# A two-layer encoder step on one core: statistics in two products at feed-forward norms, half chunks of low parts at norms, the last centrings on TensorE

## The reference

```python
h = layer_norm_0(alpha * h + 0.5 * swiglu_0(h))               # norms 0 and 3
h = layer_norm_1(alpha * h + concat(A(h), B(h), C(h), D(h)) @ w_o)   # norms 1 and 4
h = layer_norm_2(alpha * h + 0.5 * swiglu_1(h))               # norms 2 and 5
# swiglu: (silu(h @ w_gate) * (h @ w_up)) @ w_down, with 2816 hidden features
# layer_norm: (x - mean) * rsqrt(var + 1e-5) * g + b, over the 1024 features
```

## Time and profile before

| | |
|---|---|
| median of 3 runs | 1159.66 us (1159.55 to 1159.9) |
| profiled execution | 1159.8 us, span 1158.0 us |
| busy: TensorE | 1131.5 us, 98% of the span |
| busy: VectorE, ScalarE, GpSimd | 688.5, 542.7, 95.5 us |
| mean granted TensorE clock | 0.996 |

### The profile page before, as it was taken

How to read it: one execution, slowest core, us unless ns; L and a number is a source line. 1 busy time by engine, 2 the same in 40 slices (tenths; PEclk the granted TensorE clock), 3 DMA queues, 4 the chain that set the end, 5 groups by cost and what they waited for, 6 DMA issues and landing times.

```text
span 1158.0 us, 20727 instructions
## 1 busy us (share of the span) xinstructions
PE 1131.5 (98%) x8612; PEld 1098.8 (95%) x8612; DVE 688.5 (59%) x929; ACT 542.7 (47%) x770; POOL 95.5 (8%) x92
## 2 busy tenths in 40 slices
PE   9999999999998999999999999999999989999996
PEld 8999999979898999999999999999788989999995
DVE  5545545777659754445584545467867596454443
ACT  6343443464655634344464344346547564434432
POOL 1000000100153000000100000010003610000001
PEclk9999999999999999999999999999999999999998
DMA  9554444433333544444445454452433325544431
GB/s 344 183 182 149 168 158 159 149 129 99 120 125 135 179 153 177 151 158 164 147 162 199 149 181 136 164 171 95 166 114 126 127 91 201 179 150 169 164 101 41
DMA packets 28020, 177.02 MB, mean 153 GB/s; under 512 B 3312, under 2 KB 3376, under 8 KB 10288
## 3 DMA queue, kind: packets, MB, share of 16 engines
q1 hardware_dynamic: 26208, 170.18, 43.1%
q0 software_dynamic: 1744, 5.88, 1.4%
HBM read 171.79 MB, written 4.25 MB: 152 GB/s over the span
## 4 chain that ended last, share of the span: by engine, by line
PE 88%; DVE 5%; ACT 3%; issue 2%; DMA 1%; POOL 1%; SPq 0%; DVEq 0%; POOLq 0%; ACTq 0%
PE ps L475 25%; PE ps L476 25%; PE ps L477 25%; ACT w_high L1092 1%; PE ps L512 1%; PE ps L517 1%; PE ps L513 1%; DMA raw<-weights 1%; DVE w_low L1407 1%; DVE z L1559 1%; PE ps L907 1%; PE ps L906 1%; PE ps L908 1%; PE ps L864 1%; PE ps L603 1%
## 5 line engine op out<-in xcount | busy, mean ns | idle before, releaser
L475 PE MATMUL ps<-x_high,w_high 128*128 128x288 f32 x1536 | 456.3, 297 | 2.5 <-DVE w_low L1407 2.0
L1407 DVE TENSOR_TENSOR w_low<-raw,w_high 128x2048 fp32r<-128x2048 f32 (+4 forms) x151 | 328.9, 2180 | 211.0 <-ACT w_high L1092 210.6
L477 PE MATMUL ps<-x_high,w_low 128*128 128x288 f32 x1536 | 452.9, 295 | 0.0
L476 PE MATMUL ps<-x_low,w_high 128*128 128x288 f32 x1536 | 452.8, 295 | 0.0
L1092 ACT ACTIVATE w_high<-raw 128x2048 fp32r<-128x2048 f32 (+2 forms) x166 | 302.7, 1827 | 113.8 <-PE ps L477 109.1
L475 PEld LDWEIGHTS ps<-x_high,w_high 128*128 128x128 f32 x1536 | 288.5, 188 | 6.2 <-DVE w_low L1407 2.5
L477 PEld LDWEIGHTS ps<-x_high,w_low 128*128 128x128 f32 x1536 | 288.4, 188 | 0.0
L476 PEld LDWEIGHTS ps<-x_low,w_high 128*128 128x128 f32 x1536 | 288.2, 188 | 0.2
L477 PE MATMUL ps<-hid_high,w_low 128*128 128x288 f32 x704 | 208.2, 296 | 0.0
L476 PE MATMUL ps<-hid_low,w_high 128*128 128x288 f32 x704 | 208.2, 296 | 0.0
L475 PE MATMUL ps<-hid_high,w_high 128*128 128x288 f32 x704 | 208.1, 296 | 0.0
(11 more groups left out here) (311 smaller groups left out, 1141.2 us busy)
## 6 DMA issues: line engine op xcount, KB each, us to landing
raw<-weights SPq DMA_DIRECT2D x138, 1024.0 KB, 4.9
raw<-weights SPq DMA_DIRECT2D x16, 768.0 KB, 4.3
raw<-weights SPq DMA_DIRECT2D x4, 968.0 KB, 5.1
raw<-weights SPq DMA_DIRECT2D x6, 512.0 KB, 4.0
raw<-weights SPq DMA_DIRECT2D x8, 256.0 KB, 5.9
out_k<-kT POOLq DMA_DIRECT2D x2, 864.0 KB, 4.5
raw<-weights SPq DMA_DIRECT2D x2, 640.0 KB, 5.6
hT<-x_in SPq DMA_DIRECT2D x4, 288.0 KB, 5.3
```

The costliest lines, as they stand in the source:

```text
L475: pe.matmul(out, wh, xh, start=first, stop=False, skip_group_check=True)
L476: pe.matmul(out, wh, xl, start=False, stop=False, skip_group_check=True)
L477: return pe.matmul(out, wl, xh, start=False, stop=last, skip_group_check=True)
L1407: dve.tensor_tensor(wl, r, wh.bitcast(F32), ALU.subtract).then_inc(low_ready, 1)
```

## The change

- At norms 0, 2 and 3 (`sums_whole`) VectorE adds slice 7 to the sum of slices and its square to the sum of squares, and TensorE makes two products instead of four. At the mixers' norms four stay, with the mean's two ahead of the squares'.
- `EARLY_FFN` is 2 instead of 1, `EARLY_MIX` 2 instead of 3.
- In `norm`, VectorE makes only half of the next low part between the variance and the first scaled slice, and the other half after slice 3 (norms 0, 3) or 4 (norms 1, 2, 4). TensorE waits for the halves singly.
- At the mixers' norms: VectorE, not GpSimd, makes the low part of the first feed-forward chunk, ahead of slices 0 and 1. The two columns are made before any slice. The half chunk that stood after slices 2 and 3 stands ahead of slices 4 and 5; the early low parts of slices 2 and 3 move behind slice 7. ScalarE makes early high parts ahead of squares, and the third chunk's high part ahead of the mean's square.
- Norm 5: ScalarE copies minus the mean here too. TensorE centres slices 3 to 7 with two identity products each (`center_last`), and VectorE scales them from PSUM.
- The activation table of the feed-forward block is loaded at the very start, not after the first high parts.

```diff
-POOL_LOW = tuple(range(WO_AT, FFN1_AT + 1))
+POOL_LOW = tuple(range(WO_AT, FFN1_AT))
-EARLY_FFN, EARLY_MIX = 1, 3
+EARLY_FFN, EARLY_MIX = 2, 2
+BY_DVE = 3
...
+            return n in EARLY and n % 3 != 1          # sums_whole(n)
...
-                low(l, WO_AT + 4)                      # GpSimd
...
@@ TensorE, stats(n)
                 pe.wait_ge(zsum_ready, n + 1)
+                if sums_whole(n):
+                    pe.matmul(mean, ones, zsum[:, 0, :], start=True, stop=True).then_inc(mean_ready, 1)
+                    pe.wait_ge(all_squares_ready, whole_before(n) + 1)
+                    pe.matmul(square, ones, zsqsum[:, 0, :], start=True, stop=True).then_inc(stat_ready, 1)
+                    for k in range(first, KD):
+                        early_tile(n, k)
+                    return
...
+            def center_last():
+                for j in range(BY_DVE, KD):
+                    out = ps[:, last_bank(j), 0:TOK]
+                    pe.matmul(out, ident, z[:, j, :], start=True, stop=False, skip_group_check=True)
+                    if j == BY_DVE:
+                        pe.wait_ge(mean_copied, len(EARLY) + 1)
+                    pe.matmul(out, ident, minus_mean[:, :], start=False, stop=True, skip_group_check=True)\
+                        .then_inc(last_centered, 1)
...
@@ ScalarE, square(n, q), at mixers
+                        if n % 3 == 1:
+                            high_until(next_chunks(n) + NSPLIT)
@@ ScalarE, norm(n)
+                act.activation(minus_mean[:, :], stat_banks(n)[0], ACT.Copy, scale=-1.0 / D_MODEL).then_inc(mean_copied, 1)
                 if n in EARLY:
-                    act.activation(minus_mean[:, :], stat_banks(n)[0], ACT.Copy, scale=-1.0 / D_MODEL).then_inc(mean_copied, 1)
...
@@ VectorE, residual(n, q, used, after)
                 if n % 3 == 1:
                     dve.wait_ge(part_added, 4 * (n // 3) + q + 1)
+                    if q == 2:
+                        low_half(after, 0)
+                        dve.wait_ge(wo_ready, 2 * (n // 3) + 2)
...
+                    if at_ == 7 and sums_whole(n):
+                        dve.wait_ge(z_ready, 5 * (n + 1))
+                        dve.tensor_tensor(zsum[:, 0, :], zsum[:, 0, :], z[:, 7, :], ALU.add).then_inc(zsum_ready, 1)
+                        dve.wait_ge(zsqsum_ready, n + 1)
+                        dve.wait_ge(zsq_ready, 5 * (n + 1))
+                        dve.tensor_tensor(zsqsum[:, 0, :], zsqsum[:, 0, :], zsq[:, 1, :], ALU.add)\
+                            .then_inc(all_squares_ready, 1)
                 if q == 3:
                     if n % 3 == 1:
+                        early_low(n, 1)
                         early_low(n, 2)
                     early_low(n, 3)
                     low_half(after, 1)
...
-                if n % 3 == 1 and q == 1:
-                    low_half(after, 0)
-                if n % 3 != 1 or q == 1:
+                if n % 3 != 1:
                     early_low(n, q)
@@ VectorE, norm(n)
                 center(0)
                 center(1)
                 if n in EARLY:
-                    low_until(next_chunks(n) + NSPLIT)
+                    low_half(next_chunks(n) + 2, 0, half_low_ready)
                 dve.wait_ge(rstd_ready, n + 1)
                 scale(0)
                 high_first()
+                if n not in EARLY:
+                    for j in range(2, BY_DVE):
+                        center(j)
+                    for j in range(1, KD):
+                        scale(j)
+                    return
                 scale(1)
                 for j in range(2, KD):
                     center(j)
                     low(j - 2)
                     scale(j)
+                    if n in EARLY and j == (3 if which == 0 else 4):
+                        low_half(next_chunks(n) + 2, 1)
...
@@ VectorE, mixer(l)
-                low_until(base + MIX_CHUNKS + WO_CHUNKS + 1)
                 out_low(l, 2)
                 copy_t(l, 2)
                 part(l, 3)
                 out_low(l, 3)
+                dve.wait_ge(columns_ready, l + 1)
+                early_columns(3 * l + 1)
+                low_until(base + MIX_CHUNKS + WO_CHUNKS + 1)
```

More of the change, by code:

```diff
@@ L313, in down_bank, with last_bank, sums_whole, whole_before @@
             return (6, 4)[q % 2]
+        def last_bank(j):
+            return (0, 1, 6, 7, 4)[j - BY_DVE]
+        def sums_whole(n):
+            return n in EARLY and n % 3 != 1
+        def whole_before(n):
+            return sum(sums_whole(m) for m in range(n))
         def squares_added(n, q):
@@ L1065, in _ @@
                 stats(3 * l + 2)
+            center_last()
         @block.scalar
@@ L1141, in early_high, with early_columns @@
                                    scale=gb[:, n // 3, n % 3, 0, j:j + 1]).then_inc(zx_high_ready, 1)
+            def early_columns(n):
+                return act.activation(zx_high[:, :, TOK:ZW].rearrange("p k c -> p c k"), gb[:, n // 3, n % 3, :, :], ACT.Copy)
             def square(n, q):
                 act.wait_ge(z_ready, 5 * n + q + 1)
-                if q == 0:
+                if q == 0 and n % 3 == 1:
+                    early_high(n, 0)
+                    early_high(n, 1)
+                    act.activation(zsqsum[:, :, :], z[:, 0:2, :], ACT.Square).then_inc(zsq_ready, 1)
+                elif q == 0:
                     act.activation(zsqsum[:, :, :], z[:, 0:2, :], ACT.Square).then_inc(zsq_ready, 1)
@@ L1150, in square @@
                     if n in EARLY:
-                        act.activation(zx_high[:, :, TOK:ZW].rearrange("p k c -> p c k"), gb[:, n // 3, n % 3, :, :], ACT.Copy)
+                        early_columns(n)
                     early_high(n, 0)
@@ L1357, in mixer @@
                     square(3 * l + 1, q)
+            act.preload_act_table_set("silu_and_others")
             for pair in range(4):
@@ L1407, in low_part, with low_half @@
                 dve.tensor_tensor(wl, r, wh.bitcast(F32), ALU.subtract).then_inc(low_ready, 1)
-            def low_half(c, half):
+            def low_half(c, half, signal=None):
                 if c >= DEPTH * LAYER_CHUNKS:
@@ L1423, in low_half @@
                     split[0] += 1
+                elif signal is not None:
+                    ins.then_inc(signal, 1)
             def ffn(l, i):
@@ L1533, in early_low @@
                     dve.wait_ge(const_landed, 8 * 16)
-                if q == 0:
+                if q == 0 and which != 1:
                     dve.wait_ge(zx_high_ready, KD * early_before(n) + 1)
-                    dve.tensor_tensor(zx_low[:, :, TOK:ZW].rearrange("p k c -> p c k"), gb[:, l, which, :, :],
-                                      zx_high[:, :, TOK:ZW].rearrange("p k c -> p c k").bitcast(F32), ALU.subtract)
+                    early_columns(n)
                 for j in (2 * q, 2 * q + 1):
@@ L1548, in center @@
                 def center(j):
[L1550 to L1554, removed]
-                def scale(j):
-                    dve.wait_ge(centered, KD * n + j + 1)
-                    dve.scalar_tensor_tensor(out=z[:, j, :], in0=z[:, j, :], scalar=gb[:, l, which, 0, j:j + 1],
+                    dve.tensor_tensor(z[:, j, :], minus_mean[:, :], z[:, j, :], ALU.add).then_inc(centered, 1)
+                def scale(j):
+                    if n in EARLY or j < BY_DVE:
+                        dve.wait_ge(centered, KD * n + j + 1)
+                        x = z[:, j, :]
+                    else:
+                        dve.wait_ge(last_centered, j - BY_DVE + 1)
+                        x = ps[:, last_bank(j), 0:TOK]
+                    dve.scalar_tensor_tensor(out=z[:, j, :], in0=x, scalar=gb[:, l, which, 0, j:j + 1],
                                              in1=rstd[:, :], op0=ALU.mult, op1=ALU.mult).then_inc(norm_ready, 1)
```

48 lines of the change are left out of this document (34 added, 14 removed).

## The result

The changed kernel takes 1152.82 us in the median of 4 runs (1152.5 to 1153.11), the kernel before 1159.78 beside it: a ratio of 0.994, 95% interval 0.9924 to 0.9956. It is faster by 7.0 us; the forecast was 5.1, 1154.6. The time lies in the forecast's wide range (1152.5 to 1157.2), 0.3 above its lower end, and outside the narrower one that the forecast called its own (1153.6 to 1155.8). The profiled execution took 1153.06 us, span 1151.3.

A forecast was written before the change was run, and what follows sets the result against it. TensorE bounds the kernel, with an equally long VectorE path to the fifth chunk behind norms 1, 2 and 4. Terms 1.3 - 0.15 + 1.5 + 2.45 = 5.1 off 1159.66 give 1154.6 us; range 1152.5 to 1157.2, own 1153.6 to 1155.8.

The forecast's parts named there:

- The main idea: Behind norms 1, 2 and 4 VectorE's variance to fifth chunk, 24.2 us, is a second path as long as TensorE's.
- Norms 0 and 3: Two statistics products fewer save TensorE 0.97; first scaled slice comes 0.7 earlier; gain 0.65 each, bounds 0 and 0.97.
- The rotation: In the mixer behind norms 0 and 3, 1.15 of shift meets some 1.15 of slack at the first rotation product.
- Norm 2: Feed-forward to feed-forward: fifth chunk ready 0.27 later against 0.12 of slack, a loss of 0.15; bounds -0.5 and +0.3.
- Norm 5: The tail: five of eight centrings go to TensorE as ten identity products; gain 2.45, bounds 1.9 and 2.9.
- Rival (d): In the tail TensorE's clock falls to 1.2 GHz, identity products take 0.97 each: 1158.8, no change; chance 0.07.
- Norms 1 and 4: Mixer to feed-forward: VectorE takes GpSimd's 2.29 low part, yet variance comes 0.6 to 0.7 earlier; gain 0.75 each.
- the stretched price: At the mixers' norms VectorE's half chunk of low parts takes 2.50 beside GpSimd's sum, instead of 1.22 alone.
- (a): Mixers' norms give nothing: GpSimd's sums stretch early low parts too, or ScalarE's high part is late; 1156.1, chance 0.16.
- (b): Halved statistics products give nothing or cost: -0.4 for norm 2, 0 for the others; 1156.1, chance 0.16.
- (c): TensorE's idle time at mixers is wholly won, 3.3 each, as ScalarE and VectorE catch up; 1149.5, chance 0.06.
- (e): Slower: low part taken from GpSimd delays the mixers' chain by its full 2.29, 3.2 a norm; 1162.5, chance 0.05.

The follow-up runs named there:

- The late half: Changed kernel with the third chunk's whole low part between VectorE's variance and first scaled slice, instead of half there and half later: 1154.54 us.
- the shorter way: Way from variance to fifth chunk shortened behind norms 1, 2 and 4: 1149.25 us on the changed kernel, 1159.97 on the kernel before.
- norm 2's products: Norm 2 back to four statistics products and one early tile: 1152.58 us on the changed kernel, 1150.25 on the one with the shortened way.

## Why the forecast came out as it did

**The main idea held.** Behind norms 1, 2 and 4 the way over VectorE and ScalarE to the fifth chunk was as long as TensorE's. The late half (no loss there, 0.96 at norms 0 and 3), the shorter way (3.4 on one kernel, 0.2 on the other) and norm 2's products (nothing, or 0.96) each show it from another side. The stalls of 0.6 came where the forecast put them. That the total stayed within the range is in part luck: the mixers' norms won 3.4 together, where the range's lower end gave them 2.0, and the other norms and the start stayed below what that end gave them.

**Norms 0 and 3:** forecast 0.65 each, won 0.83 and 0.80, within the bounds. That is 0.15 short of the two products' 0.97, with a wait of 0.3 for the first low part of x (line 929 in the waits, 0.6 for two norms) as the forecast had it: TensorE is there 0.97 earlier, the slice a little less. The rotation had enough slack. Undone alone, the products cost 0.66 there and the half 0.96, together twice what the change won: without either edit the other wins little, so here too two ways had to be shortened together.

**Norm 2:** forecast -0.15, measured -0.21. That two products fewer win nothing there was right; that the numbers are so close is luck. The forecast's own terms give a fifth chunk 0.5 - 0.27 = 0.23 later, not 0.27. In the trace the variance is 0.40 later, but the low part behind it only 0.04 (4.85 behind slice 7 instead of 4.81), as that waited for ScalarE before; its two halves cost another 0.05 over the whole. The fifth chunk's low part and first matmul, kernel after:

```profile
598.10 2.29 DVE L1462 TENSOR_TENSOR w_low<-raw,w_high 128x2048 fp32r<-128x2048 f32 x1 [1.35 <-ACT w_high L1133]
```
```profile
600.53 0.40 PE L490 MATMUL ps<-x_high,w_high 128*128 128x288 f32 x1
```

With slice 7 at 573.12, and at 574.96 before, the low part starts 24.98 behind it instead of 24.89, 0.09 later. Its end and TensorE's first matmul are 0.14 apart here, where TensorE waited for it (the 0.22 without a name, above), and 0.18 before; so the slack was 0.04 rather than 0.12. Both terms were too large, and 0.12 of the measured loss lies behind the gating, where the forecast had nothing.

**Norm 5:** forecast 2.45, won 2.54, 2.53 by the run that undid it. Rival (d), a lower clock in the tail, didn't come: from 1141.5 to the end the granted clock was 1.00, the 2.4 GHz level, where it had been 0.63 behind TensorE's end.

**Norms 1 and 4: the step that failed is one price.** "I take the stretched price, as GpSimd starts some 0.6 us into it: 356.4" is the mis-sized term. The half took 1.23, not 2.50: the price was taken from a row in which GpSimd had started first, for a walk in which VectorE starts first. The walk up to it was right: with the 0.21 between the kernels added, slices 0 and 1 came at 349.58 (forecast 349.7) and the half at 353.83 (354.0). Then slices 4 and 5 came at 354.98 (356.4). The sum behind them gave back 0.45, as GpSimd now waits for the half and so falls on the sum; slice 7 came at 359.0 (359.95), and the variance at 363.8 (364.8). The two more early low parts cost 0.87, as forecast (0.9). So of the microsecond by which the variance was early, the half gave 1.2, of which the sum took 0.45 back, and its earlier start 0.2. This excess of 0.9 to 1.0 at each of two norms is that of the whole forecast; the start took 0.6 of it back in the profiled execution. The other parts of the change at these norms (the columns, two early tiles instead of three, ScalarE's new order, the order of the products) were not undone one by one, so what each of them is worth stays open.

Of the rivals, (a) and (b) fall with the stretches of norms 1, 4, 0 and 3. (c) was half true: 1.8 of the 3.3 us of idle time at a mixer's norm went, and of the 1.5 that is left 0.6 is the stall before the fourth chunk. (e) would have needed ScalarE's high part of the first chunk 2 us late; VectorE took it at 347.16, 347.37 on the old scale, where the forecast had 347.45.

The Trainium skill's rule, named in the forecast at that place ("SBUF — State Buffer", section "Who interferes with whom"), gave the half its 1.22, but the variance that the forecast worked out by it, 364.65, let the sum behind wait too long. The trace agrees with the rule and not with that working.

**The start** was put at nothing, and came 0.62 later in the profiled execution. ScalarE, kernel after, waits longer for the second piece of the first weights (0.31 before):

```profile
0.74 1.28 ACT L1413 ACT_TABLE_LOAD   x1 [0.74 <-PEq L2112]
...
7.25 0.63 ACT L1416 ACTIVATE w_high<-raw 128x512 fp32r<-128x512 f32 x1 [1.28 <-DMA raw<-weights]
```

Both kernels load a table at 0.74 or 0.75, and ScalarE then waits over 2 us for the first weights; the second load of the kernel before, at 13.63, is gone in the kernel after, and ScalarE waits for a DMA behind that place in both. So the table load shows no part in it, as forecast. The mark lies at 217.94 and 218.02 in the two profiles with the load in its old place, and at 217.95 to 219.15, in the middle 218.31, in the eleven with it moved; whether this is more than scatter stays open.

## What to carry to other kernels

Before pricing a saving on the busiest engine, look for whoever arrives there just in time: where a second way is as long, the saving comes back as a stall, and it becomes worth its full price once that way is shortened (norm 2's two products: nothing, then 0.96). An operation that overlaps another engine's work at a shared resource has two prices, by who starts first; a move of half a microsecond can turn one into the other, so price both orders. Moving work between two engines that hold each other up has to be priced with that interference: here VectorE, relieved of 2.29 us, had its variance only 0.30 earlier, as GpSimd's work slowed its next steps.

## What was unexpected in the hardware's behaviour

- The half low part of 128x1024 took 1.23 when it started 0.53 ahead of GpSimd's addition, 2.36 when it started 0.14 behind it; GpSimd's took 1.99 and 1.42. A delay of 0.7 so cost 1.3.
- A stall of TensorE that the waits name at 0.60 cost 0.75 between matmul starts and another 0.08 at the next one; a fifth chunk 0.22 late showed as no wait at all.
- With ten identity products and then VectorE's and ScalarE's last steps behind, the granted clock stayed at 1.00 to the end of the span, with TensorE's last product done 3.9 us ahead of it; it was 0.63 in the mean over the last 11.5 us when TensorE stopped that far ahead of the end.
